# Experts' weights in pairs of units: one transfer of 2 MiB in rows of 16 KB, for four of a layer's eight batches

## The reference

```
for layer in range(2):
    h = rmsnorm(x, mix_norm[layer])
    x = x + (mixer_ab, mixer_c)[layer](h)      # 16 heads, w_in, attention, w_out
    h = rmsnorm(x, ffn_norm[layer])
    x = x + hier_moe(h, ...)                   # group of 4, then the best 2 of its 8 experts
# hier_moe, for each of the 32 experts (group g, expert e):
    a = h @ w_gate[g, e]; u = h @ w_up[g, e]   # 1024 x 256 each
    y += (silu(a) * u * comb[:, g, e]) @ w_down[g, e]   # 256 x 1024
```

## Time and profile before

| | |
|---|---|
| runs | 630.54, 631.62, 633.85 us |
| profiled execution | 632.24 us, of which span 630.4 us |
| PE busy | 565.6 us (90%), 3800 matmul records |
| DVE / ACT / POOL busy | 182.4 / 136.0 / 6.1 us |
| DMA | 233.36 MB in 34467 packets, mean 370 GB/s |
| experts' loads of 1 MiB | 190, and 4 halves of 512 KB |
| granted clock of PE, mean | 0.968 (1 is 2.4 GHz, 0.5 is 1.2 GHz) |

### The profile page before, as it was taken

The page is one execution under the profiler, slowest core; times in us unless marked ns, Lnnn a source line. Parts: engine busy times, 40 slices in busy tenths (PEclk is TensorE's granted clock), DMA queues, the critical chain, the costliest instruction groups (busy, mean ns, idle before and its releaser), DMA issues.

```text
span 630.4 us, 9427 instructions
## 1 busy us (share of the span) xinstructions
PE 565.6 (90%) x3800; PEld 365.0 (58%) x3800; DVE 182.4 (29%) x591; ACT 136.0 (22%) x351; POOL 6.1 (1%) x25
## 2 busy tenths in 40 slices
PE   8999999998999879978699999999899986997667
PEld 8878876783555345424158876778355534533323
DVE  4334455253112012011035587415311201111011
ACT  3243546341001101101031366524100110110101
POOL 0100000000000000000010000000000000000000
PEclk9999999999999989988889999999999997998998
DMA  8999946589999999999999992548999999999994
GB/s 322 423 421 418 419 170 214 205 322 414 421 419 422 420 417 422 420 421 422 419 419 421 419 423 118 201 150 321 400 422 419 421 421 418 421 421 421 422 421 195
DMA packets 34467, 233.36 MB, mean 370 GB/s; under 512 B 3824, under 2 KB 3952, under 8 KB 7280
## 3 DMA queue, kind: packets, MB, share of 16 engines
q1 hardware_dynamic: 32544, 227.16, 88.2%
q10 hardware_dynamic: 1872, 5.51, 2.4%
HBM read 231.60 MB, written 1.05 MB: 369 GB/s over the span
## 4 chain that ended last, share of the span: by engine, by line
PE 70%; DMA 20%; DVE 4%; issue 3%; ACT 3%; SPq 0%; DVEq 0%; ACTq 0%
DMA ring<-in_moe_w_gate_up 18%; PE banks L746 15%; PE banks L957 13%; PE banks L832 8%; PE banks L939 6%; PE banks L1031 6%; PE banks L1015 6%; PE banks L792 2%; PE banks L721 2%; PE banks L820 2%; PE banks L809 2%; PE banks L898 2%; PE banks L908 1%; PE banks L949 1%; PE banks L868 1%
## 5 line engine op out<-in xcount | busy, mean ns | idle before, releaser
L957 PE MATMUL banks<-ring,desk 128*32 128x512 f32 x800 | 99.2, 620 | 17.5 <-DMA ring<-in_moe_w_gate_up 17.1
L746 PE MATMUL banks<-ring,hT 128*128 128x256 f32 x416 | 94.6, 382 | 0.0
L746 PEld LDWEIGHTS banks<-ring,hT 128*128 128x128 f32 x416 | 77.3, 190 | 13.2 <-issue 3.6
L1238 ACT ACTIVATE desk<-banks 128x256 f32<-128x256 f32 x16 | 6.1, 384 | 283.7 <-PE banks L957 283.7
L957 PEld LDWEIGHTS banks<-ring,desk 128*32 128x32 f32 x800 | 23.0, 110 | 76.2 <-issue 43.4
L939 PE MATMUL banks<-desk,hT 128*128 128x128 f32 x448 | 56.3, 287 | 10.4 <-issue 10.4
L939 PEld LDWEIGHTS banks<-desk,hT 128*128 128x128 f32 x448 | 55.7, 203 | 12.0 <-issue 11.4
L832 PE MATMUL banks<-heads,ring 128*128 128x256 f32 x256 | 61.9, 387 | 0.1
L1015 PE MATMUL banks<-ring,desk 128*32 128x512 f32 x384 | 47.0, 612 | 11.2 <-ACT desk L1240 6.7
L832 PEld LDWEIGHTS banks<-heads,ring 128*128 128x128 f32 x256 | 46.4, 190 | 12.6 <-issue 6.9
L1031 PE MATMUL banks<-desk 128*128 128x256 f32 x224 | 52.1, 386 | 0.0
(11 more groups left out here) (173 smaller groups left out, 534.8 us busy)
## 6 DMA issues: line engine op xcount, KB each, us to landing
ring<-in_moe_w_gate_up SPq DMA_DIRECT2D x100, 1024.0 KB, 26.7
ring<-in_moe_w_down SPq DMA_DIRECT2D x54, 1024.0 KB, 26.7
shared<-in_moe_w_gate_up SPq DMA_DIRECT2D x18, 1024.0 KB, 18.9
ring<-in_ab_w_in SPq DMA_DIRECT2D x8, 1024.0 KB, 18.1
xT<-in_moe_w_gate_up SPq DMA_DIRECT2D x6, 1024.0 KB, 20.5
shared<-in_moe_w_down SPq DMA_DIRECT2D x6, 1024.0 KB, 23.8
ring<-in_c_w_in SPq DMA_DIRECT2D x6, 1024.0 KB, 23.2
desk<-in_bias ACTq DMA_DIRECT2D x8, 512.0 KB, 8.1
```

The source lines that it names most:

```text
L746: ins = pe.matmul(bank2(SLAB_BANK[layer][s], NT)[:, t, :], hT[:, c, t * P:(t + 1) * P], w[:, c, :], start=(c == 0 and t == 0), stop=(c == ...
L957: ins = pe.matmul(bank(0)[j * SLOTS:(j + 1) * SLOTS, :], gathered[:, c, j * SLOTS:(j + 1) * SLOTS], w[:, j, :], start=(c == 0), stop=(c == ...
```

## The change

The experts' weights come from one tensor in HBM, `experts_d`, in place of two (gate and up, down). In it, two neighbouring units stand side by side: each of 128 rows holds 8 KB of unit 2i and then 8 KB of unit 2i+1. Units 36 to 83 of each layer are loaded two at a time: one transfer of 128 rows of 16 KB to two neighbouring places. For that the 19 ring tensors are one tensor `ring`. A pair may take neighbours in `ring` or in `shared`; `xT` and `heads` can't hold one. `place_units` picks the pair of places whose later one is free earliest. SP waits until both are free; both units share one semaphore and arrive together. All other units come one by one as before, 8 KB a row, now at a distance of 16 KB in HBM. PE's, ACT's and DVE's work and order are the same.

```diff
+TWO_FROM, TWO_TO = 3 * PER_BATCH, 7 * PER_BATCH
+def in_two(k):
+    return TWO_FROM <= k < TWO_TO
 def place_units():
...
+        second = None
         for n in range(first_unit(layer, "in"), experts + PER_ROUND):
+            two = in_two(n - experts)
             may = dict(free)
-            if experts <= n < experts + PER_ROUND - LOW:
+            if experts <= n < experts + PER_ROUND - LOW - two:
                 may.update(high)
-            s = min(may, key=lambda k: (may[k][0], k))
-            loads[s] += 1
-            where.append((s, loads[s], may[s][1]))
+            if second is not None:
+                s, second = second, None
+                signal = where[-1][1]
+            elif two:
+                first = [s for s in may if s + 1 in may and s + 1 != LOW and s + 1 < INPUT]
+                s = min(first, key=lambda k: (max(may[k][0], may[k + 1][0]), k))
+                second = s + 1
+                loads[s] += 1
+                signal = (s, loads[s])
+            else:
+                s = min(may, key=lambda k: (may[k][0], k))
+                loads[s] += 1
+                signal = (s, loads[s])
+            was = (may[s][1], may[s + 1][1]) if second is not None else (may[s][1],)
+            where.append((s, signal, was))
...
-        low = [sb(f"ring{i}", [P, UNIT]) for i in range(LOW)]
+        ring = sb("ring", [P, LOW * UNIT])
+        low = [ring[:, i * UNIT:(i + 1) * UNIT] for i in range(LOW)]
...
+        def two_of(n):
+            s = WHERE[n][0]
+            at = (s if s < LOW else s - LOW) * UNIT
+            return (ring if s < LOW else shared)[:, at:at + 2 * UNIT].rearrange("p (i n) -> p i n", i=2)
+
+        def unit_arrived(eng, n):
+            s, turn = WHERE[n][1]
+            eng.wait_ge(s_unit[s], 16 * turn)
...
-                elif was is not None:
-                    sp.wait_ge(s_used, was + 1)
+                if units:
+                    sp.wait_ge(s_used, max(units) + 1)
...
+            def load_two(n, src):
+                slots_free(n)
+                sp.dma_start(two_of(n), src).then_inc(s_unit[WHERE[n][1][0]], 16)
...
                 def expert_unit(k):
-                    b, i = divmod(k, PER_BATCH)
-                    return gate_up_d[layer, DOWN * b + i] if i < DOWN else down_d[layer, BATCH * b + i - DOWN]
+                    return experts_d[layer, k // 2, :, k % 2, :]
...
-                    load(n, expert_unit(k))
+                    if not in_two(k):
+                        load(n, expert_unit(k))
+                    elif k % 2 == 0:
+                        load_two(n, experts_d[layer, k // 2])
...
+def expert_units(gate, up, down):
+    t = np.concatenate([gate_up_units(gate, up).reshape(2, BATCHES, DOWN, P, UNIT),
+                        down_units(down).reshape(2, BATCHES, BATCH, P, UNIT)], 2)
+    return np.ascontiguousarray(t.reshape(2, PER_ROUND // 2, 2, P, UNIT).transpose(0, 1, 3, 2, 4))
```

More of the change, by code:

```diff
@@ L166, with hybrid_moe_kernel @@
 WHERE = place_units()
-def hybrid_moe_kernel(nc, xT_d, small_d, bias_d, rope_d, ab_in, ab_out, c_in, c_out, gate_up_d, down_d, out_d):
+def hybrid_moe_kernel(nc, xT_d, small_d, bias_d, rope_d, ab_in, ab_out, c_in, c_out, experts_d, out_d):
     with ExitStack() as ctx:
@@ L400, in arrived @@
             def arrived(self, eng, step, place, i):
-                s, turn, _ = WHERE[self.unit0 + PER_BATCH * place + i]
-                eng.wait_ge(s_unit[s], 16 * turn)
+                unit_arrived(eng, self.unit0 + PER_BATCH * place + i)
             def used(self, step, place, count):
@@ L601, in table_landed, with slots_free @@
                 sp.wait_ge(s_bias, 16 * (i + 1))
-            def load(n, src):
-                s, turn, was = WHERE[n]
+            def slots_free(n):
                 layer = int(n >= first_unit(1, "in"))
-                if was == "norms":
+                units = [w for w in WHERE[n][2] if isinstance(w, int)]
+                if "norms" in WHERE[n][2]:
                     sp.wait_ge(s_slab, norm_slabs_before(layer, SLABS[layer]))
@@ L609, in load @@
                         table_landed(LATER[0] + 1)
-                elif was == "pairs":
+                if "pairs" in WHERE[n][2]:
                     sp.wait_ge(s_att, PAIRS * layer + LATER[layer])
                     table_landed(LATER[0] + 2)
-                elif was == "attention":
+                if "attention" in WHERE[n][2]:
                     sp.wait_ge(s_att, PAIRS * (layer + 1))
-                elif was == "attended":
+                if "attended" in WHERE[n][2]:
                     sp.wait_ge(s_used, first_unit(layer, "experts"))
-                elif was == "input":
+                if "input" in WHERE[n][2]:
                     sp.wait_ge(s_res, 4 * layer + 3)
@@ L620, in load @@
                     table_landed(LATER[0] + 3)
-                elif was == "stream":
+                if "stream" in WHERE[n][2]:
                     sp.wait_ge(s_logit_ps, layer + 1)
-                elif was is not None:
-                    sp.wait_ge(s_used, was + 1)
+                if units:
+                    sp.wait_ge(s_used, max(units) + 1)
+            def load(n, src):
+                slots_free(n)
+                s = WHERE[n][1][0]
                 if n in HALVED:
@@ L707, in slab_arrived @@
             def slab_arrived(layer, s):
-                where, turn, _ = WHERE[first_unit(layer, "in") + s]
-                pe.wait_ge(s_unit[where], 16 * turn)
+                unit_arrived(pe, first_unit(layer, "in") + s)
             def open_slab(layer):
@@ L828, in project @@
                 pe.wait_ge(s_att, PAIRS * layer + k + 1)
-                pe.wait_ge(s_unit[WHERE[n][0]], 16 * WHERE[n][1])
+                unit_arrived(pe, n)
                 w = ring_of(n).rearrange("p (c n) -> p c n", c=2)
@@ L1703 @@
         "in_c_w_out": rows_first(i["c_w_out"][0], OUTS),
-        "in_moe_w_gate_up": gate_up_units(i["moe_w_gate"], i["moe_w_up"]),
-        "in_moe_w_down": down_units(i["moe_w_down"]),
+        "in_moe_w": expert_units(i["moe_w_gate"], i["moe_w_up"], i["moe_w_down"]),
     }
```

## The result

The changed kernel took 627.46 us in the median of 6 runs (626.36 to 628.25), the kernel before 632.32 in its 6 (630.54 to 635.20). The ratio is 0.9921, with a 95% interval of 0.9898 to 0.9944: about 5.0 us less, 3.5 to 6.4.

The account below looks back on a forecast made before the run. The bound was the saturated weight stream's delivery of unit 91 plus PE's tail, in both layers. The profiled 632.24 us less 2.5 for rows, other terms 0, gave 629.7, and 0.6 less for the median 629.1; range 626.4 to 632.8.

Parts of the forecast that it names:

- What bounds it: Both layers' expert stages: the saturated weight stream's delivery of unit 91, plus PE's tail, sets the time; attention only shifts.
- Its sign that units 88 to 91 all start earlier in layer 0: End of the experts: units 88 to 91 start some 1.2 us earlier in layer 0, still after DMA waits.
- Rows of 16 KB, 0.052 us a pair: Expert stream, units 36 to 83: fewer rows and completions save 0.052 us a pair, 2.5 us, half in each layer.
- the lower bound: Row saving from plain rates, 414 GB/s in 317.5 to 319.5 us against 420: 0.036 us a pair, 1.7 us.
- The range to 5.4 us: Upper bound of the row saving, rates divided by busy share: 0.112 us a pair, 5.4 us.
- The 2 us of fixed time a transfer: Per DMA: 48 fewer would bring 96 us if none overlapped; with engines full, none of it on the path.
- rival 3: Tails' 1.2 GHz clock dips may shift: 626 us if later or gone, 633 if longer; chance 0.12, split evenly.
- Issue and places: SP's 48 fewer issues and waits for both places cost 0; tightest, the first pair, has 7 us of cover.
- First of a pair late: Batch 7: a pair's first unit lands 2.49 us late; unit 88 up to 0.2 us late, cost 0 at unit 91.
- Single units in the new tensor: Units still loaded alone: their 8 KB rows, now 16 KB apart in HBM, cost 0.
- Rivals 1 and 2: Engines' stream: nothing saved per row, 631.5 us, chance 0.13; wide rows slower, 637.6 us at 640 ns each, chance 0.07.
- Chances: Whole time: 0.29 for faster by over 0.5%, 0.61 for within 0.5%, 0.10 for slower.

Follow-up runs that it names:

- e2_rows_8k: Changed kernel with each pair still one 2 MiB transfer, but its units stored one behind the other, so rows are 8 KB; 632.08 us, ratio 0.9984 to kernel before.
- e1_single: Changed kernel's new tensors, but every unit loaded alone in 8 KB rows; 632.99 us, ratio 1.0003 to the kernel before.
- e3_two_transfers: Changed kernel with its pairs of places and waits, but each pair as two 1 MiB transfers in 8 KB rows; 633.09 us, ratio 0.9985 to kernel before.
- e7_pairs_28_90: Changed kernel with pairs for units 28 to 89 of each layer; 626.27 us, ratio 0.9902 to the kernel before.
- e8_best: Changed kernel with pairs for units 36 to 47 and 84 to 89, fours for 48 to 83; 623.89 us, ratio 0.9870 to the kernel before.
- e5_fours: Changed kernel with units 36 to 83 loaded four at a time in 32 KB rows; 629.40 us, ratio 0.9958 to the kernel before.
- e9_pairs_to92: Changed kernel with pairs for units 36 to 91 of each layer; 626.75 us, ratio 0.9919 to the kernel before.

## Why the prediction came out as it did

The mechanism was right: fewer rows on the engines, a faster stream, an earlier unit 91. The term for it was too small, 2.5 us in place of about 3.5, and the tails gave about 1 us that the sum had at nothing.

- *What bounds it*: right. Unit 91's start moved, by 1.7 us in layer 0 and 4.1 us in layer 1 (2.3 of them carried over from layer 0), still after a wait on the DMA; attention only shifted. The rates, 425 to 427 GB/s, are at or above the 423 to 425 of the prediction. Its sign that units 88 to 91 all start earlier in layer 0 doesn't hold for unit 88: it is the fifth of the six units from 301.42 us on, so it starts at about 305.0, before at 304.83. That went with the late pair and cost nothing at unit 91.
- *Rows of 16 KB, 0.052 us a pair*: this is the term that was mis-sized. Unit 91 came 1.73 + 1.74 = 3.5 us earlier over 48 pairs, 0.072 us a pair. The rates say 0.082 in the best stretch of 70 us (4.993 against 4.911 us for 2 MiB, 3.9 us in all) and 0.059 and 0.070 over the two layers' long stretches (3.1 us in all). What misled was the lower bound: 414 GB/s from 2 us in which the halves were only part of the packets. Clean rows of 4 KB move 409, by which the same sum would have been near: 16 rows 0.135 us, 8 of them 0.068, 3.2 us. The range to 5.4 us held it. The estimate from the Trainium skill (DMA: Bandwidth & Descriptors, "Where 436 GB/s comes from") was 3.8 us, and the trace comes near it with 3.1 to 3.9. The 2 us of fixed time a transfer, which "Anatomy of one DMA" of the Trainium skill's same page gives for transfers issued from GpSimd, would have paid in `e2_rows_8k` too and did not, so with a full queue they are off the path here.
- *The other 1 to 1.5 us*: the profiled spans differ by 4.5 us, of which 3.5 are unit 91's and 1.0 are the tails behind it, 0.60 in layer 0 (from unit 91 to the next layer's first slab 14.44 us in place of 15.04) and 0.43 in layer 1. Both tails ran at 1.2 GHz for a stretch in either kernel, in layer 0 up to 320.4 us before and up to 318 now, in layer 1 up to about 621 and 615, as these stretches of the changed kernel show against the earlier trace rows. Seen from unit 91's start, the clock is back 0.7 us sooner in layer 0 (8.0 us behind it, now 7.3) and 2 us sooner in layer 1 (8.7, now 6.7); but in layer 1 it was also down sooner, so that unit 91 itself took 1.93 us in place of 1.06:

```profile
311.00:318.00 7.00, 5.51 (x44) 2.10 (x36) 0.42 (x1) 1.43 (x4) 0.00 (x0) 0.51 1.01 415
318.00:324.50 6.50, 5.95 (x54) 3.11 (x47) 2.83 (x5) 3.17 (x7) 2.84 (x12) 1.00 1.03 421
608.00:615.00 7.00, 5.22 (x36) 1.99 (x40) 0.43 (x1) 1.22 (x4) 0.00 (x0) 0.51 0.97 399
```

  That is rival 3 on its kind side, beside the forecast and not in its place. One profile of each kernel can't say that pairs cause it, since the tails differ as much among kernels without wide rows. Start of unit 91 in layer 0, of layer 1's first slab, of unit 91 in layer 1, the span, and the two tails together, in us:

| kernel | unit 91 | slab | unit 91 | span | tails |
|---|---|---|---|---|---|
| before | 312.39 | 327.43 | 612.34 | 630.4 | 33.1 |
| `e1_single` | 312.89 | 327.11 | 613.73 | 632.7 | 33.2 |
| `e3_two_transfers` | 313.11 | 327.30 | 613.49 | 631.0 | 31.7 |
| `e2_rows_8k` | 312.05 | 325.36 | 610.09 | 627.6 | 30.8 |
| changed | 310.66 | 325.10 | 608.27 | 625.9 | 32.1 |
| `e7_pairs_28_90` | 310.06 | 324.45 | 609.88 | 626.5 | 31.0 |
| `e8_best` | 309.76 | 323.08 | 605.15 | 621.8 | 30.0 |

  In the first column every kernel with wide rows is ahead of every kernel without; in the last one they mix. The clock matters in one more place: in `e1_single`, `e3_two_transfers` and `e7_pairs_28_90` PE ran two units of layer 1's first batch at 1.2 GHz, and the time from the slab to unit 91 is 1.3 to 2.3 us longer there (286.62 and 286.19 us against 284.91 in the kernel before, 285.43 against 283.17 in the changed one). Here is `e1_single`, where the units take 3.58 us and not 1.92:

```profile
438.82 3.58 PE L994 MATMUL banks<-ring,desk 128*32 128x512 f32 x16 [0.20 <-DVE desk L1593]
```

  Over all runs the clock does lean one way: the mean granted clock was 0.969 to 0.974 in the six runs of the changed kernel, and 0.956 to 0.973 (mean 0.964) in the 29 runs of the kernel before that were timed beside `e1_single`; `e2_rows_8k`, with the same joint landing, has a mean of 0.966. So part of the gain beyond the rows is probably the clock. That pairs cause it wasn't shown: no run changed the clock alone.
- *Issue and places*: 0, right (`e3_two_transfers`). The share never fell where the first pairs come. What the step said it would cost without cover, `e5_fours` showed, at twice the size I worked out for it.
- *First of a pair late*: 0 at unit 91, right (`e2_rows_8k`; PE's order above). The step left out that PE might run the pair at 1.2 GHz, which made it 1.6 us later; the waits before units 90 and 91 had room for that. The idle pieces of 3 us in batch 7 came as said (2.88).
- *Single units in the new tensor*: 0, right (`e1_single`).
- *Rivals 1 and 2* (nothing saved; wide rows slower) fell with 6912 packets fewer and 427 GB/s: a row of 16 KB takes 4.911 / 8 = 0.614 us of its engine, a completion included. The 1.2 us of a 16 KB code packet did not carry over to rows that go to SBUF.
- *Chances*: 0.61 went to within 0.5% because the term sat just under that bound (3.2 us). With the right size, 3.5 us, it sits just above it. The measured 5.0 us are twice the term, since its size and the tails erred to the same side. That the time still lay in the range, 1.1 us above its lower end, is owed to the width of the range and not to the sum.

## What to carry to other kernels

Where transfers are already 1 MiB and the engines are full, it was the length of a row that counted, not the number of transfers: each row cost its engine some 8 to 10 ns, which is 3% at 8 KB and half of that at 16 KB. To get longer rows, lay data that is used one after the other side by side in HBM and in SBUF. Before widening, follow for each wide transfer which place comes free last and when the stream gets there; the hole in `e5_fours` cost more than the wider rows gave, by the medians. And where the last microsecond matters, compare two profiles at a point ahead of the places where the clock may be down, and leave the whole time to the medians of many runs.

## What was not expected of the hardware

In both kernels PE stood still at the branch ahead of batch 5, "issue" in the profile. The changed kernel, PE in order of time:

```profile
226.73 6.58 PE L976 MATMUL banks<-desk,hT 128*128 128x128 f32 x32 [6.66 <-issue]
```

Before it was 5.13 us. That might have been instruction code held up behind wider rows, but `e1_single` with 8 KB rows alone has nearly the same:

```profile
226.44 5.78 PE L976 MATMUL banks<-desk,hT 128*128 128x128 f32 x32 [6.21 <-issue]
```

and `e7_pairs_28_90`, with more wide rows than the changed kernel, has the shortest pause of all, 4.96 us. So it varies by over a microsecond without regard to the rows. It is off the path here, since PE waits for the stream two batches later. The stream goes with it, though: in 200 to 240 us it moved 420 GB/s in the two kernels with rows of 8 KB and a pause of 5.1 us (before, `e3_two_transfers`), and 417 and 418 in the two with 6.2 us (`e1_single`, `e2_rows_8k`); with pairs it was 426 at 4.96 us (`e7_pairs_28_90`), 424 at 6.54 (`e9_pairs_to92`) and 421 at 6.66 (changed). Which of the two slows the other wasn't tried.
